# Forty modulation halves of a two-layer backbone: from TensorE matmuls to sums on VectorE inside the branch merges

## The reference

```python
silu_c, silu_cc = jax.nn.silu(c), jax.nn.silu(c_ctx)
for l in range(DEPTH):
    sh1, sc1, g1, sh2, sc2, g2 = split(silu_c @ w_mod[l] + b_mod[l], 6)           # w_mod[l]: 1024 x 6144
    csh1, csc1, cg1, csh2, csc2, cg2 = split(silu_cc @ w_mod[l] + b_mod[l], 6)
    u, uc = h * (1 + sc1) + sh1, hc * (1 + csc1) + csh1
    y, y_ctx = token_mixer(u, uc, ...)       # w_in projection, convolution, attention, mLSTM,
                                             # gated merge of three branches, output projection
    h = layer_norm(alpha * h + g1 * y)
    u2 = h * (1 + sc2) + sh2
    hc = layer_norm(alpha * hc + cg1 * y_ctx); uc2 = hc * (1 + csc2) + csh2       # not in the last layer
    f = grouped_moe(tokens)                  # 16 experts, top 1 group, top 2 experts in it
    h, hc = layer_norm(alpha * h + g2 * f_lat), layer_norm(alpha * hc + cg2 * f_ctx)
```

## Time and profile before

| | |
|---|---|
| profiled execution, device time | 1651.09 us |
| its span, first to last instruction | 1649.3 us |
| median of three runs | 1651.62 us |
| TensorE busy | 1555.0 us (94%) |
| VectorE busy | 765.5 us (46%) |
| ScalarE busy | 373.1 us (23%) |
| GpSimd busy | 219.2 us (13%) |
| read from HBM | 356.66 MB |

### The profile page before, as it was taken

One profiled execution on the slowest core, in us unless ns is written; L12 is line 12 of the kernel. 1 busy time (PEld: TensorE's weight loads), 2 busy tenths in 40 slices (PEclk: granted clock), 3 DMA queues, 4 the chain that ended last, 5 costly groups with the idle time before them and its releaser, 6 DMA issues.

```text
span 1649.3 us, 32450 instructions
## 1 busy us (share of the span) xinstructions
PE 1555.0 (94%) x13532; PEld 979.6 (59%) x13532; DVE 765.5 (46%) x1542; ACT 373.1 (23%) x894; POOL 219.2 (13%) x239
## 2 busy tenths in 40 slices
PE   6999999999999999899999896999999998999985
PEld 3454475565444458665666454767678887566642
DVE  3159924475101113653336546396553126654555
ACT  1100035742000010422222122002652002122211
POOL 0200000000000000033334321000000000444421
PEclk9999999999999999999999998999999999999998
DMA  9634657602223141699679999452224667999993
GB/s 331 177 102 144 205 181 252 221 27 82 99 67 115 56 161 51 225 407 406 245 272 397 406 404 350 153 139 66 73 51 155 207 217 256 380 407 407 407 408 151
DMA packets 175107, 365.30 MB, mean 221 GB/s; under 512 B 14337, under 2 KB 93801, under 8 KB 174451
## 3 DMA queue, kind: packets, MB, share of 16 engines
q1 hardware_dynamic: 162400, 330.43, 55.0%
q0 software_dynamic: 10112, 27.06, 4.9%
q10 hardware_dynamic: 2451, 5.73, 1.2%
HBM read 356.66 MB, written 10.62 MB: 223 GB/s over the span
## 4 chain that ended last, share of the span: by engine, by line
PE 58%; SPq 8%; DVE 5%; DMA 4%; ACT 2%; issue 1%; DVEq 0%; POOLq 0%; ACTq 0%
PE psum L1154 56%; SPq L964 8%; DMA uT<-in_moe_w_gu 2%; DMA yab<-in_moe_w_gu 1%; PE psum L1692 1%; DMA ys<-qkT,y_row 1%; PE psum L1444 0%; DMA convT<-us,x_row 0%; PE psum L1262 0%; DMA yab<-ys 0%; DVE st L2186 0%; DVE ring L2738 0%; DVE H L2761 0%; DVE st L2187 0%; DVE H L2199 0%
## 5 line engine op out<-in xcount | busy, mean ns | idle before, releaser
L1154 PE MATMUL psum<-uT,ring 128*128 128x512 f32 (+1 forms) x1440 | 493.5, 500 | 3.9 <-ACT uT L1857 2.1
L1154 PEld LDWEIGHTS psum<-uT,ring 128*128 128x128 f32 x1440 | 272.1, 191 | 212.5 <-issue 192.2
L1154 PE MATMUL psum<-ring,mo_tok 128*32 128x256 f32 x4992 | 315.6, 386 | 18.5 <-DVE ring L2738 18.4
L1154 PEld LDWEIGHTS psum<-ring,mo_tok 128*32 128x32 f32 x4992 | 155.1, 111 | 128.2 <-DVE ring L2738 32.2
L1154 PE MATMUL psum<-ring,v_tok 128*32 128x256 f32 x2496 | 149.9, 381 | 0.6 <-ACT v_tok L2106 0.6
L2343 DVE SCALAR_TENSOR_TENSOR convT<-upad,cwT,convT 128x512 f32<-128x512 f32 (+1 forms) x240 | 132.4, 614 | 2.1
L1154 PEld LDWEIGHTS psum<-ring,v_tok 128*32 128x32 f32 x2496 | 81.3, 111 | 55.8 <-issue 2.4
L1154 PE MATMUL psum<-ring,uT 128*128 128x256 f32 (+1 forms) x576 | 113.6, 358 | 0.0
L1154 PEld LDWEIGHTS psum<-ring,uT 128*128 128x128 f32 x576 | 99.2, 191 | 16.5 <-issue 5.4
L2560 DVE TENSOR_TENSOR arena<-psum,mqk 128x512 f32<-128x512 f32 (+1 forms) x16 | 8.9, 558 | 205.9 <-PE psum L1154 205.9
L1154 PE MATMUL psum<-yab,ring 128*128 128x512 f32 (+1 forms) x256 | 85.2, 486 | 0.0
(11 more groups left out here) (361 smaller groups left out, 1557.9 us busy)
## 6 DMA issues: line engine op xcount, KB each, us to landing
ring<-in_w_in SPq DMA_DIRECT2D x104, 512.0 KB, 4.8
ring<-in_w_mod SPq DMA_DIRECT2D x84, 512.0 KB, 7.2
yab<-in_moe_w_gu SPq DMA_DIRECT2D x44, 512.0 KB, 16.0
uT<-in_moe_w_gu SPq DMA_DIRECT2D x43, 512.0 KB, 14.0
arena<-in_moe_w_gu SPq DMA_DIRECT2D x41, 512.0 KB, 15.4
mqk<-in_moe_w_gu SPq DMA_DIRECT2D x25, 512.0 KB, 15.8
mv_tok<-in_moe_w_gu SPq DMA_DIRECT2D x24, 512.0 KB, 12.4
yab<-in_moe_w_dn SPq DMA_DIRECT2D x24, 512.0 KB, 11.6
```

The costliest lines, as they stand in the source:

```text
L1154: return nc.tensor.matmul(dst, lhsT, rhs, start=start, stop=stop)
```

## The change

All 40 later halves leave TensorE's `modulation`. They are summed by VectorE after the merge steps of layer 0: for each 128x512 part `q` of a half one operation, accumulator = weights * (one conditioning value per partition) + accumulator. Units whose modulation both streams need (12 of the 20) take it twice, into two accumulators, so there are 256 operations of 128x512 in all; `link` makes VectorE wait for its own result after each part. There are 32 sums (`SUMS`) in eight buffers (`sum_bufs`). TensorE then adds a sum's 128 partitions: `add_partitions` takes four sums with four 128x32 matmuls, eight such batches in all, seven in the merge and one behind the first output product. `HALVES_AT_MERGE` gives the halves behind each merge step.

The weights of these halves no longer pass through the ring: GpSimd's queue loads them, two DMAs of 512 KB a half, into two buffers in turn (`values` and `convT`); the load of a half waits until the half two before it is summed. Two groups of columns remain where there were four: group 2 (12 halves, behind merge step 4) and group 3 (28 halves, behind the second output product). The staging buffers `values0` and `values1` come free later and stand further back in `STAGES`, the wait of `rows` is another, and the last two gathers before layer 1 no longer wait for the border's halves.

```diff
 MOD_GROUPS = [
     [(0, 0), (0, 2)],
     [(0, 1), (0, 3)],
-    [(0, u) for u in range(4, 12)],
-    [(1, u) for u in (0, 1, 2, 3, 6, 11)],
-    [(1, u) for u in (4, 5, 10)],
-    [(1, u) for u in (7, 8, 9)],
+    [(0, u) for u in range(4, 10)],
+    [(0, 10), (0, 11)] + [(1, u) for u in range(12)],
 ]
+BOTH_STREAMS = [(0, u) for u in range(4, 12)] + [(1, u) for u in range(4)]
+SUMS = [(x, c) for x in SUMMED_UNITS for c in range(2 if x in BOTH_STREAMS else 1)]
+SUM_BATCH = 4
+SUM_BUFS = 2 * SUM_BATCH
+HALVES_AT_MERGE = (5, 5, 5, 5, 8, 11, 1, 0)
+BATCHES_AT_MERGE = {1: (0,), 2: (1,), 3: (2,), 4: (3, 4), 5: (5,), 6: (6,)}
+COLUMNS_MERGE = 4
...
-MOD_SPOTS = ([("mqk", t) for t in range(1, 8, 2)] + [("mv", c, 1) for c in range(2)] + [("mo", c, 1) for c in range(2)]
-             + [("step", i) for i in (1, 2, 3, 4, 5, 6, 7, 9, 11, 13, 15, 17)])
...
+            def load_halves_to_sum():
+                for at, (m, u, half) in enumerate(SUMMED_HALVES):
+                    if at == 1:
+                        wait_ready(pool, "yc", 0, NH - 1)
+                    if at >= 2:
+                        pool.wait_ge(summed, at - 1)
+                    for g in range(2):
+                        pool.dma_start(sum_rows[at % 2][:, 2 * g:2 * g + 2, :],
+                                       wmod[m][:, 4 * half + 2 * g:4 * half + 2 * g + 2, u * 512:(u + 1) * 512])\
+                            .then_inc(sum_loaded[at % 2], 16)
...
+                def add_partitions(batch):
+                    sums = SUMS[SUM_BATCH * batch:SUM_BATCH * (batch + 1)]
+                    pe.wait_ge(summed, 2 * SUMMED_UNITS.index(sums[-1][0]) + 2)
...
+                    for q, (x, c) in enumerate(sums):
+                        row = 2 * MOD_GROUPS[mod_group(*x)].index(x) + c
+                        last = mm(psum[MOD_BANK][32 * q:32 * q + 32, :], one_column[:, 31 - row:63 - row],
+                                  sum_bufs[sum_of(x, c) % SUM_BUFS], batch in (0, FIRST_BATCHES),
+                                  batch in (FIRST_BATCHES - 1, N_BATCHES - 1))
+                    last.then_inc(mod_used, 1)
...
+                def sum_half(x):
+                    m, u, half = x
+                    streams = [c for y, c in SUMS if y == (m, u)]
+                    at = SUMMED_HALVES.index(x)
+                    dve.wait_ge(sum_loaded[at % 2], 32 * (at // 2 + 1))
+                    if half == 0 and sum_of((m, u), 0) >= SUM_BUFS:
+                        dve.wait_ge(mod_used, halves_to(FIRST_GROUPS - 1) + sum_of((m, u), 0) // SUM_BATCH - 1)
+                    for q in range(4):
+                        for c in streams:
+                            acc = sum_bufs[sum_of((m, u), c) % SUM_BUFS]
+                            w, scale = sum_rows[at % 2][:, q, :], cT[:, 4 * half + q, MOD_AT + c:MOD_AT + c + 1]
+                            if (half, q) == (0, 0):
+                                last = v.tensor_scalar(acc, w, scale, None, ALU.mult)
+                            else:
+                                last = v.scalar_tensor_tensor(acc, w, scale, acc, ALU.mult, ALU.add)
+                        if q < 3:
+                            link(last)
+                    last.then_inc(summed, 1)
+                    dve.wait_ge(summed, at + 1)
                 for j in range(KD):
                     ...
+                    for x in halves_at_merge(l, j):
+                        sum_half(x)
+                    if (l, j) == (0, COLUMNS_MERGE):
+                        modulation(2)
...
-                    for t in range(2):
+                    for t in range(nt):
                         gather_tile(t)
                     act.wait_ge(rows_used, 2 * l + 2)
                     gate_rows(1)
-                    act.wait_ge(mod_used, halves_to(5))
-                    for t in range(2, nt):
-                        gather_tile(t)
-                    keep_rows(5)
```

More of the change, by code:

```diff
@@ L103, in halves_to, with mod_uses, gate_group, halves_at_merge @@
     return sum(len(halves) for halves in MOD_HALVES[:g + 1])
-def gate_groups(layer):
-    return (2,) if layer == 0 else (3, 4)
-def in_pairs(halves):
-    return [halves[i:i + 2] for i in range(0, len(halves), 2)]
-MOD_SPOTS = ([("mqk", t) for t in range(1, 8, 2)] + [("mv", c, 1) for c in range(2)] + [("mo", c, 1) for c in range(2)]
-             + [("step", i) for i in (1, 2, 3, 4, 5, 6, 7, 9, 11, 13, 15, 17)])
-MOD_SPREAD = dict(zip(MOD_SPOTS, in_pairs(MOD_HALVES[2]) + [[x] for x in MOD_HALVES[3]]))
-assert len(MOD_SPOTS) == len(MOD_SPREAD)
-COLUMNS_STEP, COLUMNS_UNIT = 2, len(UNITS)
-def mod_at(layer, *spot):
-    return MOD_SPREAD.get(spot, []) if layer == 0 else []
+def mod_uses(g):
+    return halves_to(min(g, FIRST_GROUPS - 1)) + (0, 0, FIRST_BATCHES, N_BATCHES)[g]
+def gate_group(layer, which):
+    return 2 if (layer, which) == (0, 0) else 3
+def halves_at_merge(layer, j):
+    first = sum(HALVES_AT_MERGE[:j])
+    return SUMMED_HALVES[first:first + HALVES_AT_MERGE[j]] if layer == 0 else []
+assert sum(HALVES_AT_MERGE) == len(SUMMED_HALVES)
+def sum_of(x, c):
+    return SUMS.index((x, c))
 BRANCHES = ("bga", "bgb", "bgc")
@@ L333, in psum_order @@
             order += [("PV", l, i // 2 - 2)] if i % 2 == 0 and 0 <= i - 4 < n else []
-            order += [("modt", 2)] if l == 0 and i == COLUMNS_STEP else []
         order += [("cols", l)]
@@ L339, in psum_order @@
             order += [("kq", l, i // 2, s) for s in range(TT)] if i % 2 == 0 and i < n else []
-            order += [("modt", 3)] if l == 0 and i == COLUMNS_UNIT else []
         spread = len(SPREAD_GATES[l]) // len(BRANCHES)
@@ L600, in build @@
         sig = mqk
+        sum_bufs = [extra[:, 0:512], extra[:, 512:1024], qkT[:, 4, :], qkT[:, 5, :]]
+        sum_bufs += [ln_rows[:, x * 512:(x + 1) * 512] for x in range(SUM_BATCH)]
+        sum_rows = [values[:, 0:4 * 512].rearrange("p (k n) -> p k n", k=4), convT[:, :, :]]
         spread_rows = [[qkT[:, 4, :], qkT[:, 5, :], upad_flat[:, 3 * T:4 * T]],
@@ L619, in build @@
         mod_used, mod_kept = sem("modulation_half_used"), sem("modulation_rows_kept")
+        summed = sem("modulation_half_summed")
+        sum_loaded = [sem(f"modulation_half_to_sum_loaded{u}") for u in range(2)]
         loaded = [sem(f"slot_loaded{s}") for s in range(NS)]
@@ L660, in build @@
         partners_loaded = sem("partners_loaded")
-        border_loaded = [sem(f"border_modulation_half_loaded{x}") for x in range(len(BORDER))]
         w_used = [sem(f"expert_part_used{x}") for x in range(NX)]
@@ L767, in used_modulation @@
                 stream.append((("mod",) + x, mod_used, MOD_ORDER.index(x) + 1))
-            def used_pair(pair):
-                for x in pair:
-                    used_modulation(x)
             def used_gates(c):
@@ L812, in build @@
                 used(("out", l, c), out_user(l, c))
-            for x in MOD_HALVES[4] if l == 0 else []:
-                used_modulation(x)
             for x in range(NS):
@@ L924, in wait_stage_free @@
             def wait_stage_free(l, name):
-                if name.startswith("values"):
+                if name.startswith("values") and l == 0:
+                    sp.wait_ge(summed, len(SUMMED_HALVES))
+                elif name.startswith("values"):
                     wait_ready(sp, "hv", l, len(UNITS) - 1, token_tiles(l) // 2 - 1)
@@ L1006, in _ @@
                     at += NS
-                    for x in range(len(BORDER) if l == 0 else 0):
-                        load_border(x)
                 else:
@@ L1535, in _ @@
                         done(last, key, l, j)
+                    for batch in BATCHES_AT_MERGE.get(j, ()) if l == 0 else ():
+                        add_partitions(batch)
+                    if (l, j) == (0, COLUMNS_MERGE):
+                        modulation_columns(2)
                     if j + GATES_AHEAD[l] < KD:
@@ L1539, in gate_rows @@
                 def gate_rows(which, first):
-                    for g in gate_groups(l):
-                        wait_drained(pe, "modt", g)
+                    wait_drained(pe, "modt", gate_group(l, which))
                     for c in range(nt):
@@ L2083, in _ @@
                     natural(t)
[L2085 to L2087 removed]
+                if l:
                     gate_rows(1)
```

144 lines of the change are left out of this document (48 added, 96 removed).

## The result

| kernel | median us | lowest to highest | ratio to the kernel before, 95% interval |
|---|---|---|---|
| before | 1654.4 | 1650.6 to 1658.0 | |
| changed | 1674.5 | 1673.6 to 1677.7 | 1.0131, 1.0107 to 1.0154 |

The change costs 1.3%, some 20 us; the profiled executions are 1651.1 and 1673.9 us, 22.8 apart. The forecast was 1649, the range ended at 1666.

The account below looks back on a forecast made before the run. TensorE, busy 94% of the span, was taken to bound the kernel. Savings of 36.1 us less 33.9 for the merges and what follows gave 2.2 back from 1651.1, so 1649; range 1633 to 1666.

Parts of the forecast that it names:

- What TensorE gets back ahead of the merges: Projections 14.8 us, first half of the steps 1.8, steps 2 to 17 10.5, plus one group's columns: 28.0 us saved.
- The third rival: Attention steps: ScalarE's chain bounds them once the halves are out, so 4 us back instead of 10.5; 1655, 12%.
- The experts' start, 4.0: Experts' first weights: without 6 MB of halves ahead, loads come some 15 us earlier, 4.0 us back, else 0.
- Between the layers, 2.3 and the columns of one group: Between the layers: last stores and gather shorten without the border's 6 MB, 2.3 us; with one group's columns, 3.2 back.
- Eighth batch, columns, cold start, 4.7: Output projection: eighth batch and columns cost 2.0 us, restart at half clock behind TensorE's 18 us idle costs 2.7.
- A sum, 0.69 us: VectorE in the merges: 0.69 us an operation, so 5.4 us a half for two streams, 2.9 for one.
- The rate, (load + sum) / 2, and TensorE's own 218.3: Merges: two buffers give 5.5 us a two-stream half, 4.25 a one-stream half; TensorE itself would be through at 218.3.
- A load, 5.6 us everywhere: GpSimd's loads of the halves in the merges: 5.6 us each, between 5.0 and 7.2, DMA engines being 72% free.
- So steps 0 to 3 hold: Merge steps 0 to 3: five halves of 5.5 us behind each merge end 39.5 us into a step, in time.
- The wait at batches 3 and 4 within a microsecond: Merges: TensorE's wait at these batches for the twentieth half is within a microsecond.
- the second, the slow loads in steps 4 and 5: Rival, GpSimd's queue there: 7.2 us a load makes the merges cost 43.7 us instead of 26.7; 1666, 20%.
- The first (loads keep pace): Rival, merges: loads keep up, VectorE's own pace counts, stage 218.4 us, no idle stretch or cold start; 1628, 14%.

Follow-up runs that it names:

- no_sums: Changed kernel with the loads and sums of the 40 halves left out, except two loads and eight plain products; 1634.4 us, 0.9886 of the kernel before.
- one_stream_sums: Changed kernel with all 40 loads, but each half of the 24 for two streams summed for one stream only; 1657.4 us, 1.0018 of the kernel before.
- three_buffers: Changed kernel with a third buffer for the halves, so two loads are under way while a half is summed; 1640.0 us, 0.9922 of the kernel before.
- one_load: Changed kernel with all sums, but only the first two halves loaded and all 40 summed from these buffers; 1632.2 us, 0.9871 of the kernel before.
- drain_early: Changed kernel with VectorE taking up the first summed group's columns behind the first of merge 4's eight halves, not the last; 1675.9 us.
- half_loads: Changed kernel with only the first of the two 512 KB DMAs issued for each half from the third on; 1658.4 us, 1.0037 of the kernel before.

## Why the prediction was wrong, step by step

- *What TensorE gets back ahead of the merges* (14.8 + 1.8 + 10.5 + the columns of one group): right. 28.6 us measured, 28.0 forecast. The third rival (attention gives little) is out with that.
- *The experts' start, 4.0*: right in sign, too small. 6.4 us measured. The kernels with none, six and eight halves in the routing (281, 287 to 289, 292 us) speak for its cause, the halves' 6 MB there; it was not tried by itself.
- *Between the layers, 2.3 and the columns of one group*: right, 3.5 against 3.2. The two kernels with halves there take 21.9 and 23.6 us, those without 18.3 to 18.7.
- *Eighth batch, columns, cold start, 4.7* and *routing, 2.5 less the columns of one group*: right, 5.0 and 1.6. Without the idle stretch ahead of it (no_sums) the output projection to the count takes 75.5 instead of 79.1, so by this difference the cold start is 3.6 of the 5.0, more than the 2.7 forecast.
- *A sum, 0.69 us*: nearly. The operations took 0.75 (a chained one 0.78 from start to start), the plain products 0.49, so a half some 5.55 and 3.0 us instead of 5.4 and 2.9. Over 24 and 16 halves that is 5.2 us of VectorE's time.
- *The rate, (load + sum) / 2, and TensorE's own 218.3*: right. The first is borne out by one_stream_sums and three_buffers, the second by no_sums' 218.5.
- *A load, 5.6 us everywhere*: the step that failed. In quiet stretches it was right (5.6 to 5.7 us from first issue to use). In step 5, where it counts most, eleven halves took 625.4 - 566.3 = 59.1 us where the forecast had 44.0. The nine of them that VectorE waited for took 8.2 us each on average from first issue to use, 10.3 and 11.8 at worst; 8.2 instead of 5.6 is 11 x 2.6 / 2 = 14.3 us, nearly all of the 15.1 lost there. I took the DMA share of the whole stretch, 28% of the earlier trace rows, as room at every moment. But SyncE's loads come in bursts, and the same stretch holds the output projection's eight DMAs and the first expert weights, which were in front of me.
- *So steps 0 to 3 hold*: true of TensorE (step 4 began at 127.2 us, forecast 126.6), not of VectorE, and it failed by the same step. The first 20 halves took 6.0 us each instead of 5.5, with three loads of 7.4 to 9.5 us beside the ring's weights, and merge 4 began 7.8 us late. In one_load, without the waits, it began when forecast.
- Together: VectorE waited 42.9 us for loads where the forecast's sums held 20.0, and its sums took 5.2 us more; 2.2 us of that fell into a pause that the forecast had ahead of merge 4. 22.9 + 5.2 - 2.2 = 25.9, the miss within 0.2 us.
- *The wait at batches 3 and 4 within a microsecond*: wrong, 4.1 us, since VectorE was late with the twentieth half; and the one of 7.34 us for a PSUM bank that VectorE drained only behind merge 4's halves was not seen at all. By drain_early neither cost anything.
- *The rivals*: the second, the slow loads in steps 4 and 5, is what happened in kind, and it had 20%. In size it was too small in step 5 (52.6 us for its eleven halves, measured 59.1) and in its lag of 2 us ahead of step 4 (7.8), and too large in step 4 itself (46.4, measured 42.9). Its 1666 was the range's end, 8 us short. The first (loads keep pace) is what one_load makes of the kernel: its stage of 218.4 was 221.1 there.

On the two rules that stand beside the prediction's loads: GpSimd's issues of the halves' loads took 0.71 to 0.76 us in all 80 cases, 0.72 also at 373.98, where VectorE stood idle. The contention that the Trainium skill describes (SBUF — State Buffer, "SBUF: two separate sides") does not show on these issues. It may show on the row that the prediction took: the same issue for `norm_g`, 0.92 us beside VectorE's TENSOR_SCALAR in the earlier trace rows, took 0.56 at 1033.28, where no TENSOR_SCALAR ran. Where an issue of a half ran beside two plain products, three times in 12 pairs the products were longer, 1.09 to 1.12 us for the pair instead of 0.88, which is under 1 us in all. One issue of step 5 came 1.75 us late (the chain above) beside operations with two tensor inputs. The Trainium skill (VectorE: DVE Perf Modes, "Why `tensor_tensor` can't do 2×_2P or 4×") says that `tensor_tensor` has no two-port mode, since it needs the second port for its second tensor. If that holds for these operations too, a two-port mode is not what delayed the issue, and what did stays open.

## What to carry to other kernels

The lesson is to price a new transfer at the moment it runs, not by the mean DMA share of its stage: look for the queue's own bursts there, and take the crowded duration for those that lie on the chain. When work is handed to an idle engine with two load buffers, the pace is (transfer + work) / 2, so the shorter the work, the more it is the transfer's; a third buffer took 34 of 43 us of waiting away here, and no bandwidth had been missing. A wait of TensorE in the middle of a stage costs nothing when another engine's chain sets the stage's end: what counts is which chain ends last.

## What the runs showed of the hardware

- A DMA of 512 KB through GpSimd's queue landed 4.1 us after its issue at the least (half_loads); in a pair, a second one issued 0.72 us later added 1.5 (5.6 to 5.7 in the changed kernel). The Trainium skill (DMA: Bandwidth & Descriptors, "Anatomy of one DMA — SWDGE (gpsimd) path") gives about 2.0 us and the bytes at 436 GB/s, by which 512 KB would take an estimated 3.2; here it was never under 4.1, the issue's own 0.71 included.
- Beside other transfers the same pair took 6.9 to 11.8 us; the stretches read around those over 7 us have a DMA share of 0.87 to 1.06.
- The earlier trace rows repeated itself: in 1033.86 to 1038.00, behind 14.5 us of idle time, TensorE ran at a granted clock of 0.50, the lower of its two levels (1.2 GHz), though busy nearly throughout.

```profile
1033.86:1038.00 4.14, 3.89 (x17) 3.60 (x18) 3.85 (x5) 0.82 (x3) 0.92 (x1) 0.50 1.08 374
```

- Layer 1, nearly the same program in all kernels, took from 633.5 to 642.0 us in their traces, so in a stage that long some 4 us to either side can't be read from one trace of each. The experts' stage repeated itself more closely: 280.8 to 281.2 in the five complete kernels without halves in the routing.
